# A transformer block in fp32: router logits and first gate taken from rows that the norm's root has not scaled yet

## The reference, cut to what matters

```python
x = x + concatenate([y_pool, y_attn]) @ w_out
h = rms_norm(x, norm_ffn)
aff = softmax(h @ w_router)                    # 512 x 16
gates, idx = top_k(aff.T, 64)                  # every expert chooses 64 rows
ye = (silu(h[idx] @ w_gate) * (h[idx] @ w_up)) @ w_down   # 16 experts, 2048 wide
x = x + zeros.at[idx].add(ye * gates)
g = sigmoid(rms_norm(x, norm_ple) @ w_ple_gate)
e = rms_norm(p @ w_ple_proj, norm_ple_post)
x = x + g * e
```

## Time and profile before

| | us |
|---|---|
| median of 3 runs | 2095.17 (2094.62 to 2095.71) |
| the profiled execution's own time | 2097.64 |
| its span in the trace | 2095.8 |
| PE busy | 1948.5 (93%) |
| DVE busy | 845.4 (40%) |
| ACT busy | 572.8 (27%) |

### The profile page before, as it was taken

How to read it: one execution, slowest core, us unless ns; L and a number is a source line. 1 busy time by engine, 2 the same in 40 slices (tenths; PEclk the granted TensorE clock), 3 DMA queues, 4 the chain that set the end, 5 groups by cost and what they waited for, 6 DMA issues and landing times.

```text
span 2095.8 us, 23298 instructions
## 1 busy us (share of the span) xinstructions
PE 1948.5 (93%) x9049; PEld 1139.0 (54%) x9049; DVE 845.4 (40%) x1273; ACT 572.8 (27%) x901; POOL 37.3 (2%) x40
## 2 busy tenths in 40 slices
PE   7989899999999999999999987999999999999898
PEld 6656633322222222222222266888888788778786
DVE  6874621111111111111110166456466576876443
ACT  4453410000000000000000044443133433357651
POOL 1023000000000000000000000000000000000000
PEclk9998999999999999999999999999999999999999
DMA  8422399999999999999999953445345232211101
GB/s 258 161 93 73 156 361 421 422 421 422 422 422 422 422 421 422 422 422 422 422 422 422 420 184 118 167 161 192 114 143 181 81 94 87 81 61 41 41 21 41
DMA packets 132179, 528.11 MB, mean 252 GB/s; under 512 B 10006, under 2 KB 55892, under 8 KB 82836
## 3 DMA queue, kind: packets, MB, share of 16 engines
q1 hardware_dynamic: 129492, 520.56, 63.0%
q0 software_dynamic: 1008, 3.52, 0.7%
q10 hardware_dynamic: 1616, 3.15, 0.4%
HBM read 524.97 MB, written 2.23 MB: 252 GB/s over the span
## 4 chain that ended last, share of the span: by engine, by line
PE 53%; DMA 35%; DVE 6%; ACT 3%; issue 1%; SPq 1%; ACTq 0%; DVEq 0%
DMA w_expert<-in_w_up 17%; DMA w_expert<-in_w_gate 16%; PE bank L1085 6%; PE bank L889 5%; PE bank L890 5%; PE bank L891 5%; PE bank L868 5%; PE bank L869 5%; PE bank L870 5%; PE bank L908 1%; PE bank L1095 1%; DMA raw<-in_w_ple_gate 1%; SPq L714 1%; PE bank L1303 1%; DVE full L1772 1%
## 5 line engine op out<-in xcount | busy, mean ns | idle before, releaser
L1085 PE MATMUL bank<-w_expert,chosen 128*64 128x512 f32 x2048 | 483.7, 602 | 62.0 <-DMA w_expert<-in_w_up 45.7
L1085 PEld LDWEIGHTS bank<-w_expert,chosen 128*64 128x64 f32 x2048 | 130.4, 136 | 395.4 <-issue 232.9
L1954 DVE TENSOR_TENSOR x_res<-x_res,bank 128x512 f32<-128x512 f32 x136 | 87.3, 684 | 428.4 <-PE bank L1104 408.1
L1095 PE MATMUL bank<-w_expert,hidden_t 128*64 128x512 f32 x1024 | 229.9, 596 | 5.9 <-ACT hidden_t L1515 4.6
L1709 DVE TENSOR_TENSOR w_lo<-raw,w_hi 128x2048 fp32r<-128x2048 f32 x75 | 171.9, 2292 | 156.5 <-ACT w_hi L1350 156.5
L1350 ACT CAST w_hi<-raw 128x2048 fp32r<-128x2048 f32 x75 | 142.8, 1904 | 152.9 <-PE bank L891 136.4
L868 PE MATMUL bank<-act_hi,w_hi 128*128 128x512 f32 x424 | 173.4, 409 | 0.1
L1976 DVE TENSOR_TENSOR hidden_rows<-gate_silu,bank 128x512 f32<-128x512 f32 x32 | 20.6, 684 | 364.1 <-PE bank L1085 364.1
L870 PE MATMUL bank<-act_hi,w_lo 128*128 128x512 f32 x424 | 166.1, 392 | 0.0
L869 PE MATMUL bank<-act_lo,w_hi 128*128 128x512 f32 x424 | 166.0, 391 | 0.0
L1095 PEld LDWEIGHTS bank<-w_expert,hidden_t 128*64 128x64 f32 x1024 | 74.6, 137 | 138.7 <-issue 121.1
(11 more groups left out here) (287 smaller groups left out, 2484.7 us busy)
## 6 DMA issues: line engine op xcount, KB each, us to landing
w_expert<-in_w_gate SPq DMA_DIRECT2D x128, 1024.0 KB, 24.9
w_expert<-in_w_up SPq DMA_DIRECT2D x128, 1024.0 KB, 26.5
w_expert<-in_w_down SPq DMA_DIRECT2D x128, 1024.0 KB, 26.5
raw<-in_a_w_in SPq DMA_DIRECT2D x24, 1024.0 KB, 6.3
raw<-in_b_w_in SPq DMA_DIRECT2D x16, 1024.0 KB, 5.2
raw<-in_a_ada_w SPq DMA_DIRECT2D x12, 1024.0 KB, 5.3
raw<-in_b_ada_w SPq DMA_DIRECT2D x12, 1024.0 KB, 6.3
raw<-in_kv_ada_w SPq DMA_DIRECT2D x8, 1024.0 KB, 5.8
```

Of the source, the lines that this page charges most:

```text
L1085: last = mm(PS[b0 + n][HALF[x], :], XE[:, k % 4, HALF[k // 4]], WE[place][:, r], start=(k == 0), stop=(k == KD - 1), skip_group_check=True)
L1095: last = mm(PS[4][HALF[x], :], HT[:, 2 * q + k, HALF[half]], WE[place][:, r], start=(i == 0 and k == 0), stop=(i == 7 and k == 1), skip_gr ...
L1954: tt(part, part, ps[:, :], ALU.add).then_inc(d_add, 1)
```

## The change

In stage 1 the rows go to the router without the root. DVE writes `x_norm` = x * gain for each column half right behind the add. PE turns tile t into two banks (`turn_rows`), tiles 0 and 1 already inside the output product, ahead of the products of tiles 2 and 3 of its last half, tiles 2 and 3 behind it. ACT copies the first bank of each tile, DVE the second, to the four places. The router's products are done tile by tile (eight chunks of 128 rows instead of eight of 512). The squares go to a scratch place, and one mean, one root and one reciprocal serve all four tiles. The logits are multiplied by the root on DVE before the softmax. ACT scales the rows of `x_norm` by the root after the exponential, and PE waits for that before the first gather. ACT loads the exponential's table behind the copy of the logits.

In stage 3 PE turns `X` itself, in chunks 0 to 3 and 4 to 7, as soon as the adds allow. The adds stand together, `w_lo` behind them, then the low parts. Squares, mean, root and reciprocal come after the splits of the chunks; the root is the scale of the sigmoid.

The diff, without semaphore names and most unchanged lines:

```diff
@@ -332,9 +332,6 @@
                 count["lo"] += k in (3, 4, 5)
-            if k == 1:
-                note(("logits",), "act")
-                note(("logits_t",), "dve")
@@ -380,10 +377,15 @@
                 note(("wout", h, t), "dve")
+                for u in ((), (0,), (1,), (2, 3))[t] if h else ():
+                    note(("turn", u, 0), "act")
+                    note(("turn", u, 1), "dve")
                     note(("pt", c), "lo")
-        note_norm(1)
+        note(("logits",), "act")
+        note(("logits_t",), "dve")
@@ -605,7 +608,20 @@
-        XT4, LGT = [FULL[0][:, :], FULL[1][:, :], SQ[0][:, :], SQ[1][:, :]], FULL[0][:, :]
+        JOINT, UNSCALED, BY_BOTH = (1, 2), (2,), ()
+        def small_step(k, t):
+            return sum(1 if j in JOINT else NT for j in range(k)) + (1 if k in JOINT else t + 1)
+        def rows_scaled(k, t):
+            if k in BY_BOTH and t % 2:
+                return n_xa, t // 2 + 1
+            per = [0 if j in UNSCALED else 2 if j in BY_BOTH else NT for j in range(k)]
+            return n_xn, sum(per) + (t // 2 if k in BY_BOTH else t) + 1
+        XT4, LGT = [FULL[0][:, :], FULL[1][:, :], SQ[0][:, :], SQ[1][:, :]], at("logits_turned", 130, [P, S])[:, :]
@@ -836,16 +852,17 @@
                 banks = []
-                for chunks in (range(0, 6), range(6, KD)):
-                    if k == 2:
-                        pe.wait_ge(d_add, ADDS - 2 if chunks[0] == 0 else ADDS)
+                for chunks in (range(0, 4), range(4, KD)) if k == 2 else (range(0, 6), range(6, KD)):
                     for t in range(NT):
-                        pe.wait_ge(n_xn, 4 * min(k, 4) + t + 1)
+                        if k == 2:
+                            pe.wait_ge(d_add, ADDS - 8 + max(chunks[-1] + 1, 2 * t + 2))
+                        else:
+                            pe.wait_ge(*rows_scaled(min(k, 4), t))
                             last = nc.tensor.transpose(grid_tile(banks[kc], t) if k == 0 else banks[kc][:, t * P:(t + 1) * P],
-                                                       XNORM[k][:, t, kc * P:(kc + 1) * P], ident)
+                                                       (X if k == 2 else XNORM[k])[:, t, kc * P:(kc + 1) * P], ident)
@@ -870,7 +887,7 @@
-            def tm_unit(ws, keys, ah, al, f0=None, halves=(0, 1), between=None):
+            def tm_unit(ws, keys, ah, al, f0=None, halves=(0, 1), between=None, ahead=None):
@@ -878,6 +895,8 @@
                             banks.append(begin(keys[t], ends_next=False))
+                        elif ahead is not None:
+                            ahead(t)
@@ -998,10 +1017,24 @@
+            def turn_rows(t):
+                pe.wait_ge(*rows_scaled(1, t))
+                for x in range(2):
+                    b = begin(("turn", t, x))
+                    for k in range(4):
+                        last = nc.tensor.transpose(b[:, k * P:(k + 1) * P], XNORM[1][:, t, (4 * x + k) * P:(4 * x + k + 1) * P],
+                                                   ident)
+                    last.then_inc(filled, 1)
+            def turn_first_rows(t):
+                if t >= 2:
+                    turn_rows(t - 2)
                         (lambda kc: 13 + kc if kc < 4 else 5 + kc) if h == 0 else None, (1, 0),
-                        pooled_products if h == 0 else None)
+                        pooled_products if h == 0 else None, turn_first_rows if h else None)
@@ -1012,18 +1045,24 @@
             pe.wait_ge(s_wr, 16)
-            norm(1)
-            lg = begin(("logits",))
-            for kc in range(KD):
-                pe.wait_ge(freed["act"], fills[("norm", 1, kc)][2])
-                part = slice(kc % 4 * 32, (kc % 4 + 1) * 32)
-                last = mm(lg[part, :], WR[:, kc, :], XT4[kc % 4], start=(kc < 4), stop=(kc >= 4), skip_group_check=True)
-                if kc < 4:
-                    last.then_inc(r_used, 1)
-            last.then_inc(filled, 1)
-            pe.wait_ge(freed["act"], fills[("logits",)][2])
+            turn_rows(2)
+            for t in range(NT):
+                if t == 2:
+                    turn_rows(3)
+                if t == 0:
+                    lg = begin(("logits",), ends_next=False)
+                pe.wait_ge(freed["act"], fills[("turn", t, 0)][2])
+                pe.wait_ge(freed["dve"], fills[("turn", t, 1)][2])
+                for kc in range(KD):
+                    part = slice(kc % 4 * 32, (kc % 4 + 1) * 32)
+                    last = mm(lg[part, t * P:(t + 1) * P], WR[:, kc, :], XT4[t % 2 * 2 + kc // 4][:, kc % 4 * P:(kc % 4 + 1) * P],
+                              start=(kc < 4), stop=(kc >= 4), skip_group_check=True)
+                last.then_inc(r_used if t < NT - 1 else filled, 1)
+            ends(("logits",))
             for t in range(NT):
+                if t == 0:
+                    pe.wait_ge(freed["act"], fills[("logits",)][2])
@@ -1109,6 +1148,7 @@
             pe.wait_ge(d_sel, 1)
+            pe.wait_ge(s_xr, NT)
@@ -1331,7 +1371,7 @@
-        JUNK = at("junk", 148, [P, D])
+        JUNK = at("junk", 197, [P, D])
@@ -1360,8 +1400,15 @@
                                          ).then_inc(n_sq, 1)
-                    act.wait_ge(n_ms, 4 * k + t + 1)
+                    act.wait_ge(n_ms, small_step(k, t))
                     nc.scalar.activation(STD[:, t:t + 1], MS[:, t:t + 1], ACT.Sqrt).then_inc(n_sqrt, 1)
+            def square_row(k, t, junk):
+                nc.scalar.activation(junk, X[:, t, :], ACT.Square, accum_out=SS[:, t:t + 1]).then_inc(n_sq, 1)
+            def roots(k):
+                act.wait_ge(n_ms, small_step(k, 0))
+                nc.scalar.activation(STD[:, :], MS[:, :], ACT.Sqrt).then_inc(n_sqrt, 1)
@@ -1466,18 +1513,30 @@
             split_upto(W_OUT[1][1] + 1)
-            stats(1, lambda t: (freed["dve"], fills[("wout", 1, t)][2]))
+            def turned_rows(t):
+                if t == 0:
+                    act.wait_ge(f_lo, f[0])
+                if t >= 2:
+                    act.wait_ge(r_used, t - 1)
+                nc.scalar.copy(XT4[t % 2 * 2], take(("turn", t, 0))[:, :]).then_inc(freed["act"], 1)
+            for t in range(NT):
+                act.wait_ge(freed["dve"], fills[("wout", 1, t)][2])
+                if t:
+                    act.wait_ge(n_sq, 4 + t)
+                square_row(1, t, JUNK[:, :])
+                if t:
+                    turned_rows(t - 1)
+            turned_rows(NT - 1)
+            roots(1)
+            nc.scalar.copy(LGT, take(("logits",))[:, :]).then_inc(freed["act"], 1)
             tables(ACT.Exp)
-            for kc in range(KD):
-                b = take(("norm", 1, kc))
-                if kc == 0:
-                    act.wait_ge(f_lo, f[0])
-                if kc >= 4:
-                    act.wait_ge(r_used, kc - 3)
-                nc.scalar.copy(XT4[kc % 4], b[:, :]).then_inc(freed["act"], 1)
-            nc.scalar.copy(LGT, take(("logits",))[:, :]).then_inc(freed["act"], 1)
-            act.wait_ge(freed["dve"], fills[("logits_t",)][2])
+            act.wait_ge(s_shift, 1)
             nc.scalar.activation(LGX[:, :, :], LGX[:, :, :], ACT.Exp).then_inc(k_exp, 1)
+            act.wait_ge(n_rstd, small_step(1, 0))
+            for t in range(NT):
+                act.wait_ge(filled, fill_no(("turn", t, 1)))
+                nc.scalar.activation(XNORM[1][:, t, :], XNORM[1][:, t, :], ACT.Identity, scale=RSTD[:, t:t + 1]).then_inc(s_xr, 1)
@@ -1520,9 +1579,12 @@
             split_upto(W_PGATE[0][0])
-            stats(2, lambda t: (d_add, 8 * NE + 2 * t + 2))
             split_upto(W_PGATE[0][1])
+            act.wait_ge(d_add, ADDS)
+            for t in range(NT):
+                square_row(2, t, XNORM[2][:, t, :])
+            roots(2)
@@ -1533,7 +1595,9 @@
                         act.wait_ge(x_upd, i - 1)
-                    nc.scalar.activation(SQ[i % 2][:, :], b[:, :], ACT.Sigmoid).then_inc(freed["act"], 1)
+                    if i == 0:
+                        act.wait_ge(n_rstd, small_step(2, 0))
+                    nc.scalar.activation(SQ[i % 2][:, :], b[:, :], ACT.Sigmoid, scale=RSTD[:, t:t + 1]).then_inc(freed["act"], 1)
@@ -1716,19 +1780,21 @@
-                i, one = 4 * k + t + 1, slice(t, t + 1)
-                dve.wait_ge(n_sq, i)
+                i, one = small_step(k, t), slice(t, t + 1)
+                dve.wait_ge(n_sq, 4 * k + t + 1)
                 dve.wait_ge(n_rstd, i)
-                if k == 1:
-                    if t == 0:
-                        dve.wait_ge(s_grow, 16)
-                    stt(out=XNORM[k][:, t, :], in0=X[:, t, :], scalar=RSTD[:, one], in1=GROW[:, :],
-                        op0=ALU.mult, op1=ALU.mult).then_inc(n_xn, 1)
-                else:
-                    ts(XNORM[k][:, t, :], X[:, t, :], RSTD[:, one], None, ALU.mult).then_inc(n_xn, 1)
+                ts(XNORM[k][:, t, :], X[:, t, :], RSTD[:, one], None, ALU.mult).then_inc(n_xn, 1)
+            def means(k):
```

(33 more changed lines are left out.)

3 lines of the change are left out of this document (2 added, 1 removed).

## The result

| | before | after |
|---|---|---|
| median, us | 2095.44 (2094.62 to 2099.28, 4 executions) | 2081.61 (2080.67 to 2082.43, 4 executions) |
| profiled execution, own time / span | 2097.64 / 2095.8 | 2082.43 / 2080.6 |
| ratio of the medians' runs | | 0.9926 (95%: 0.9912 to 0.994) |

The change gains 15.5 us by the ratio (12.6 to 18.4). The forecast was a gain of 9.4, to 2085.8, with a range from 2081.5 to 2092.0. So the direction was right and the size too small.

The account below looks back on a forecast made before the run. Stage 2's loads follow stage 1's chain to the first expert product, and DVE bounds stage 3. Stage 1's 1.2 + stage 3's 8.3 - 0.1 for the sigmoid = 9.4; 2095.17 - 9.4 = 2085.8 us, range 2081.5 to 2092.0.

Parts of the forecast that it names:

- Stage 2 is set by its loads, and its end follows the first expert product: Stage 2: 384 loads of 2.485 us each set its length; its end follows the first expert product one for one.
- The turns inside the output product cost 1.0 each, PE waits 0.2, the last add comes 2.2 later: Stage 1, output product: eight transposes a turn at 0.125 make 1.0; PE waits 0.2; last add 2.2 later.
- A router tile costs 1.1, bounds 0.86 to 2.2: Stage 1, router: eight products of one tile take 1.1 us, four tiles 4.4; bounds 0.86 and 2.2.
- rival A: Stage 1, router: tiles bound by instructions, 2.2 each; stage 1 loses 3.2, time 2090.2; chance 0.13.
- The product with the root costs 0.25 on the chain: Stage 1: multiplying the logits by the root adds a DVE operation, 0.25 with the wait; net gain 1.2.
- The table load is covered by 0.6, scalings and copies hide: Stage 1, ACT: the exponential's table load of 1.28 is covered by 0.6; row scalings, 4.5, hide behind DVE's search.
- Rival E: Stage 1: the clock falls in the router and stays low through the projection; slower, 2102.5; chance 0.03.
- The gather may run at the upper level, up to 2.9; taken as nothing: Stage 1, gather: may run at the clock's upper level, at most 2.9 gained of 6.29; counted as nothing.
- rival D: Stage 1: the gather runs at the clock's upper level, time 2082.9; chance 0.04.
- Stage 3: first gate product 8.0 behind the first add, 8.3 gained: Stage 3: DVE is the bound; first gate product 8.0 after the first add instead of 15.9; gain 8.3 (8.0 to 8.7).
- Rival B: Stage 3: the clock is at its lower level when the gate starts; gain there 5.3, time 2088.8; chance 0.14.
- rival C: Stage 3: root comes late, `w_lo` ready no earlier than before, PE waits 2.0; time 2087.8; chance 0.05.

Follow-up runs that it names:

- e10: Kernel before, with DVE taking the odd ones of the eight copies of turned chunks ahead of the router's products; ratio to before 0.9989.
- e9: Changed kernel with all eight products of a router tile in one column group of PE instead of four; ratio to before 0.9947.
- e5: Changed kernel once more, no instruction different; ratio to before 0.9932.
- e19: Changed kernel a fourth time, no instruction different; ratio to before 0.9933.
- e17: Changed kernel a third time, no instruction different; ratio to before 0.9931.
- e1: Kernel before with only ScalarE's scratch tile JUNK at its new address, no work moved; ratio to before 0.9996.
- e3: Gate's part of the change alone: router as before, stage 3 as in the changed kernel; ratio to before 0.9961.
- e11: Changed kernel with ACT's four squares of norm 2 ahead of its high parts of the turned x; ratio to before 0.9952.
- e12: Changed kernel with both idle PE stretches of the head filled by products whose result is overwritten; ratio to before 0.9924.
- e14: Changed kernel with the low part of the first gate slab computed by POOL instead of DVE; ratio to before 0.9927.
- e2: Router's part of the change alone: stage 3 as in the kernel before; ratio to before 0.9977.
- e6: Changed kernel with filler products for PE's two idle head stretches, those for the second running after it; ratio to before 0.9935.

## Why the prediction was right or wrong

- *Stage 2 is set by its loads, and its end follows the first expert product.* Right within 2 us: 935.9 to 937.9 in the table, wherever it started.
- *The turns inside the output product cost 1.0 each, PE waits 0.2, the last add comes 2.2 later.* Right: 8.96 us from first to last add (221.87, 230.83) instead of 6.69, 2.27 more; a turn is 0.87 to 1.09, and PE waits 0.27 for the first.
- *A router tile costs 1.1, bounds 0.86 to 2.2.* This is the step that failed. It measured 0.50, below the lower bound, and rival A with 2.2 was further off still. Two things were wrong in it. I divided 4.23 by four as if that row were PE's price; e10 shows that copies and their places stretched it. And the lower bound came from expert products that use two groups of 64 columns, while the router's neighbours use four groups of 32: e9 shows 1.80 us in one group, of which four side by side make 0.50. Half of the 0.86 that two groups gave, 0.43, would have been near. Four tiles at 0.5 instead of 1.1, without the 0.3 for changes of mode, are 2.7 less; the wait of 0.37 for DVE's last copy, which I had hidden, gives some of it back. Logits: forecast 1.5 earlier, measured 3.6, so the step is worth 2.1. (The Trainium skill, "TensorE: Matmul & The Clock Gate", section "Part 3: Packing small matmuls — row/col tiling", has products on different tiles of the array run concurrently, 2.38 times as fast for three column tiles; the 3.6 times of e9, with four, agree in kind.)
- *The product with the root costs 0.25 on the chain.* Right: 0.24 at 237.25. From first add to exponential it is 16.15 instead of 19.32, so 3.2 net where I had 1.2.
- *The table load is covered by 0.6, scalings and copies hide.* Right: 0.79 idle behind the load, so nothing else of it came due there; the scalings end at 242.4 and the gather starts at 257.1. Rival E's fall did come, but behind the router: the clock was at 0.50 from 236.9 to 243.7 (in before from 245.4 to 248.8), beside the search on DVE, and the projection was done at 252.7, ahead of the ranks at 255.2. It cost nothing that the chain shows.
- *The gather may run at the upper level, up to 2.9; taken as nothing.* In after it took 5.37 for 6.29, 0.9 less, with the clock at 0.50 from 257.4 to 260.8, where before had it from 262.4 to 269.3. So rival D came in part. The same program took 5.37 in e5 and e19 too, and 6.14 in e17; e1 and e3 took 6.2, and e11 and e12, at 1.00 all through, 3.67. I took nothing, which is near for one of the four profiles of the changed kernel and 0.9 too little for three; it is a matter of the clock in the single run, and whether the change favours it is open.
- *Stage 3: first gate product 8.0 behind the first add, 8.3 gained.* Right: 7.88, and 8.0 gained, with DVE as the bound (e14). Rival B (the clock) did not come: PEclk is 1.00, and e11 shows that it does when the high parts are late. The squares have a pitch of 1.04, not 1.25, and the third gate slab is ready at 1225.7, 5.4 before PE wants it (3.9 forecast), so rival C did not come either.
- *The sum.* By its own steps 1.2 + 8.3 - 0.1 = 9.4. The fixed part measured 3.2 + 8.0 = 11.2 to the exponential and gate product, 11.6 to the logits' copy. The mis-sized tile is 2 of the missing 4.6 to 6 us. The gather is 0.9 in three of four profiles. The remaining 2 to 3 us the forecast put at nothing, as head and later stages have the same code in both; that they are there stays without a shown cause.
- *What the range left out.* Its lower end was worked out from D with the tile at 0.86, 2085.8 - 2.9 - 1.0 = 2081.9, and 0.4 more of stage 3; with the tile at 0.50 it would have been 1.4 lower. I took three executions within 1.1 us as the spread. More executions of the same kernel spread over 10, and the profile of before was one with the fall of the clock, which I did not know for a matter of luck. The changed kernel's four measurements gain 14.0 to 15.5, the two parts alone 4.8 and 8.2. Between these and 11.6 lie 1.4 to 3.9 us that the traces show only in stretches that scatter (head, gather, last stages). That these favour the changed program on average is argued from few profiles, not shown; with the idle stretches filled in both kernels the difference is 11.4 to 12.5, some 3 either way. One more number on record speaks for it weakly: the clock granted over a whole execution. Its mean on one chip was 0.9834 in before, 0.9837 in e1, 0.9843 in e2 and 0.9852 in e3, and among executions of before the shorter ones had the higher clock. For e3 that is in line with the fall that stage 3 no longer has; for e2 it is hardly clear of the scatter, and where it would come from is not known.

## What to carry to other kernels

Before a row's length is used as a price, look whether its instructions waited for one another's data: products that wait for copies have the copies' pace. A small product's price depends on which column groups its neighbours write, so its bounds must come from rows with the same sharing. And microseconds that move in code that no edit touches are first to be looked for in a second profile of the same kernel.

## What was not expected of the hardware

- Eight products of 128 columns and 32 outputs take 0.50 us in four column groups and 1.80 in one; the order 0,4,1,5,2,6,3,7 took 0.52.
- One program, two heads: behind 2.2 us of idle PE the clock stayed at 1.00 (first add at 221.87) or went to 0.50 from 181.0 to 187.9 (226.11). In e6 it went to 0.50 at 161.0 with PE shown busy, just behind products of one column.
- POOL subtracts 2048 columns in 4.55 us beside DVE's adds, and these keep their 4.87.
